# Ten up pairs ahead of the gate rows, three behind them, and two pairs gated out of their staging tiles

## The reference

```
sc = einsum("bshpc,hpnc->bshpn", q, sub_keys)        # scores of two key halves
v1, i1 = top_k(sc[..., 0, :], 16);  v2, i2 = top_k(sc[..., 1, :], 16)
top, ci = top_k(v1[..., :, None] + v2[..., None, :], 16)
idx = i1[ci // 16] * 128 + i2[ci % 16];  g = softmax(top)
a = einsum("td,ted->te", x, u[idx])
out = einsum("te,ted->td", g * gelu(a), v[idx])
```

## Time and profile before

| | |
|---|---|
| median of 3 runs | 4096.4 us (4095.26 to 4104.18) |
| the profiled execution | 4095.76 us, span 4093.7 us |
| PE busy | 3953.3 us, 97% of the span |
| DVE, ACT, POOL busy | 68%, 43%, 28% |
| mean granted TensorE clock | 0.985 of full |

### The profile page before, as it was taken

How to read it: one execution, slowest core, us unless ns; L and a number is a source line. 1 busy time by engine, 2 the same in 40 slices (tenths; PEclk the granted TensorE clock), 3 DMA queues, 4 the chain that set the end, 5 groups by cost and what they waited for, 6 DMA issues and landing times.

```text
span 4093.7 us, 59435 instructions
## 1 busy us (share of the span) xinstructions
PE 3953.3 (97%) x19746; PEld 3399.3 (83%) x19746; DVE 2796.2 (68%) x4541; ACT 1748.0 (43%) x3160; POOL 1153.4 (28%) x786
## 2 busy tenths in 40 slices
PE   7999999989999999999999999999899999999998
PEld 6677887789999988887866778877899999888886
DVE  2584351698887977777736843427988879677786
ACT  3533123225666654333346321322356666444343
POOL 1014563411211432222200155733011224222231
PEclk9999999999999999999999999999999999999999
DMA  3112332237877999999721122312478879999995
GB/s 125 48 64 81 104 104 70 95 106 249 297 283 280 392 375 345 347 347 343 275 77 48 62 92 103 119 57 89 152 245 291 289 281 405 371 345 349 347 357 183
DMA packets 360976, 879.48 MB, mean 215 GB/s; under 512 B 27856, under 2 KB 191952, under 8 KB 353872
## 3 DMA queue, kind: packets, MB, share of 16 engines
q1 hardware_dynamic: 153360, 508.21, 34.8%
q0 software_dynamic: 73728, 268.47, 17.2%
q10 hardware_dynamic: 133696, 100.67, 8.2%
HBM read 774.48 MB, written 102.76 MB: 214 GB/s over the span
## 4 chain that ended last, share of the span: by engine, by line
PE 77%; DVE 10%; DMA 3%; issue 3%; DVEq 2%; ACTq 2%; ACT 2%; POOL 0%; SPq 0%; POOLq 0%
PE ps L1223 44%; PE ps L1533 21%; PE ps L1510 3%; DMA raw<-in_experts 2%; PE ps L1236 1%; PE ps L1244 1%; ACTq L507 1%; PE ps L1285 1%; DVE wlo L807 1%; DVE acc L1092 1%; DVE ubuf L1085 1%; DMA act_e<-early_gelu 1%; PE ps L1303 1%; PE ps L1296 1%; PE ps L1295 1%
## 5 line engine op out<-in xcount | busy, mean ns | idle before, releaser
L1223 PE MATMUL ps<-xhi,whi 128*128 128x384 f32 (+1 forms) x3264 | 1189.7, 364 | 42.0 <-DVE inds L1070 14.0
L1223 PE MATMUL ps<-xlo,whi 128*128 128x384 f32 (+1 forms) x3264 | 1164.1, 357 | 0.0
L1223 PE MATMUL ps<-xhi,wlo 128*128 128x384 f32 (+1 forms) x3264 | 1164.1, 357 | 0.0
L476 ACT ACTIVATE whi<-raw 128x1024 fp32r<-128x1024 f32 x666 | 698.3, 1054 | 362.8 <-PE ps L1533 268.9
L807 DVE TENSOR_TENSOR wlo<-raw,whi 128x1024 fp32r<-128x1024 f32 x512 | 622.2, 1218 | 161.0 <-ACT whi L476 156.9
L1223 PEld LDWEIGHTS ps<-xhi,whi 128*128 128x128 f32 x3264 | 618.0, 189 | 100.2 <-issue 36.8
L1223 PEld LDWEIGHTS ps<-xlo,whi 128*128 128x128 f32 x3264 | 618.1, 189 | 51.0 <-issue 5.3
L1223 PEld LDWEIGHTS ps<-xhi,wlo 128*128 128x128 f32 x3264 | 616.9, 189 | 48.9
L1533 PE MATMUL ps<-whi,eh 128*128 128x512 f32 x1536 | 601.6, 392 | 26.3 <-DVE el L1184 26.1
L436 POOL DMA_INDIRECT ubuf<-in_up_rows,gidx x256 | 290.6, 1135 | 1100.6 <-DVE small L1085 913.2
L1533 PE MATMUL ps<-whi,el 128*128 128x512 f32 x1536 | 599.8, 391 | 0.0
(11 more groups left out here) (216 smaller groups left out, 4879.3 us busy)
## 6 DMA issues: line engine op xcount, KB each, us to landing
raw<-in_experts SPq DMA_DIRECT2D x512, 512.0 KB, 6.4
raw<-in_back SPq DMA_DIRECT2D x112, 512.0 KB, 3.2
gate_table<-gbuf SPq DMA_DIRECT2D x48, 1024.0 KB, 6.6
act_e<-early_gelu ACTq DMA_DIRECT2D x128, 384.0 KB, 7.2
gtile<-gate_table ACTq DMA_DIRECT2D x30, 1536.0 KB, 23.3
raw<-in_front SPq DMA_DIRECT2D x64, 512.0 KB, 3.2
raw<-in_gates SPq DMA_DIRECT2D x48, 512.0 KB, 3.2
early_gelu<-weighted SPq DMA_DIRECT2D x128, 192.0 KB, 5.2
```

What stands on the lines that cost most here:

```text
L476: A(whi[:, SLOT[s]:SLOT[s] + 1024], raw[:, SLOT[s]:SLOT[s] + 1024], ACT.Copy).then_inc(rounded[s], 1)
L1223: ins = MM(out, w[:, a:a + P], x[:, c, t0:], start=(i == 0 and n == 0), stop=(i == len(chunks) - 1 and n == 2))
```

## The change

`LEAD` goes from 12 to 10, and three pairs instead of one follow the last block (`EARLY - 3`, `EARLY - 2`, `EARLY - 1`), so the gate rows come two pairs sooner. The panels of up weights are rotated by two pairs on the host, so that the last two up pairs, 62 and 63, are down pairs 0 and 1. They are neither stored nor loaded: DVE multiplies them with the gates straight out of `weighted` and of `early0`/`early1`. ACT rounds the first product (`round_share`) between the Gelus of pairs 62 and 63, and PE computes pair 63 into banks 0 and 1. SP's gate store now comes ahead of the early stores of its iteration.

```diff
-LEAD = 12
+LEAD = 10
+HELD = 2
+STORED = EARLY - HELD
+assert LEAD % 2 == 0 and LEAD + DB * BLOCK + 3 == EARLY
...
+        def up_bank(i, m):
+            return {EARLY - 1: 0}.get(i, 4) + m
...
-                        eng.dma_start(early_d[2 * i + m], early(i, m)).then_inc(...)
+                        eng.dma_start(early_d[2 * (i + HELD) + m], early(i, m)).then_inc(...)
...
                 for i in range(EARLY):
                     for m in range(2):
                         stream(2 * i + 4 + m)
-                    if i:
-                        store_early(i - 1)
                     b, k = divmod(i - LEAD - 3, BLOCK)
                     if i >= LEAD + 3 and k < HALVES and k % 2 == 0:
                         store_gates(b * GROUPS + k // 2)
-                store_early(EARLY - 1)
+                    if 1 <= i <= STORED:
+                        store_early(i - 1)
                 for s in range(4):
-                    eng.wait_ge(early_stored[s], (L + 1) * (EARLY // 2 * 16))
+                    eng.wait_ge(early_stored[s], (L + 1) * (STORED // 2 * 16))
...
                 for i in range(LEAD):
                     early_pair(i)
-                    if i == 2 or i == LEAD - 3:
+                    if i == 2 or i == LEAD - 2:
                         pick_weights(int(i > 2))
-                    if i == LEAD - 2:
-                        pick_turn(1)
+                pick_turn(1)
...
                         load_gates(L * 0, 0, 22, 24)
-                        load_acts(L * 0, 0)
                         load_gates(L * 0, 1)
-                        load_acts(L * 0, 1)
-                        early_pair(i + HALVES + 1)
+                        load_acts(L * 0, HELD)
+                        load_acts(L * 0, HELD + 1)
+                early_pair(EARLY - 3)
+                early_pair(EARLY - 2)
+                round_share(L * 0, 0)
+                early_pair(EARLY - 1)
...
-                for m in range(2):
-                    hold(early_stored[m], (L + 1) * (EARLY // 2 * 16))
                 for r in range(PAIRS):
...
+                    if r == 0:
+                        for m in range(2):
+                            hold(early_ready[m], (L + 1) * EARLY - 1)
+                        TT(by_group(weighted[:, :, :]), by_group(weighted[:, :, :]), gates, ALU.mult).then_inc(w_ready, 1)
+                    elif r == 1:
+                        for m in range(2):
+                            dve.wait_ge(early_ready[m], (L + 1) * EARLY)
+                            ins = TT(by_group(weighted[:, m:m + 1, :]), by_group(early_odd[m][:, :].unsqueeze(1)), gates[:, m:m + 1], ALU.mult)
+                        ins.then_inc(w_ready, 1)
...
-                with pe.Fori(0, LEAD // 2 - 1) as i:
+                with pe.Fori(0, LEAD // 2) as i:
                     for k in range(2):
                         early_pair(i * 2 + k, k, i)
-                early_pair(LEAD - 2, 0, LEAD // 2 - 1)
                 turn(1)
-                early_pair(LEAD - 1, 1, LEAD // 2 - 1)
...
-                early_pair(EARLY - 1, 1, EARLY // 2 - 1)
+                early_pair(EARLY - 3, 1, EARLY // 2 - 2)
+                early_pair(EARLY - 2, 0, EARLY // 2 - 1)
                 pe.wait_ge(g_copied, (L + 1) * (DB * P // 4))
-                for m in range(2):
-                    pe.wait_ge(early_ready[m], (L + 1) * EARLY)
+                early_pair(EARLY - 1, 1, EARLY // 2 - 1, up_bank(EARLY - 1, 0))
```

More of the change, by code:

```diff
@@ L358, in store_early @@
                         eng.wait_ge(early_ready[m], L * EARLY + (i + 1))
-                        eng.dma_start(early_d[2 * i + m], early(i, m)).then_inc(early_stored[2 * (i % 2) + m], 16)
+                        eng.dma_start(early_d[2 * (i + HELD) + m], early(i, m)).then_inc(early_stored[2 * (i % 2) + m], 16)
                 def store_gates(y):
@@ L687, in early_pair @@
                         panel(n % 4, L, FIRST + n // 4)
-                        act.wait_ge(early_stored[n % 4], (L * (EARLY // 2) + i // 2) * 16)
-                        A(early(i, m), ps[:, 4 + m, 0:DT], ACT.Gelu).then_inc(early_ready[m], 1)
+                        act.wait_ge(early_stored[n % 4], (L * (STORED // 2) + i // 2) * 16)
+                        A(early(i, m), ps[:, up_bank(i, m), 0:DT], ACT.Gelu).then_inc(early_ready[m], 1)
                         round_panel(n % 4, L, FIRST + n // 4 + 1)
@@ L754, in _, with round_share @@
                         load_gates(L * 0, 0, 22, 24)
-                        load_acts(L * 0, 0)
                         load_gates(L * 0, 1)
-                        load_acts(L * 0, 1)
-                        early_pair(i + HALVES + 1)
+                        load_acts(L * 0, HELD)
+                        load_acts(L * 0, HELD + 1)
+                def round_share(j, r):
+                    act.wait_ge(w_ready, L * PAIRS + j * STEPS + (r + 1))
+                    A(eh[:, r % 2, :, :], weighted[:, :, :], ACT.Copy).then_inc(eh_ready, 1)
+                early_pair(EARLY - 3)
+                early_pair(EARLY - 2)
+                round_share(L * 0, 0)
+                early_pair(EARLY - 1)
                 def steps(j, first, last):
@@ L767, in steps @@
                                 round_panel(s, L, j * (STEPS // 2) + (FIRST + PAIRS // 2 + r // 2))
-                        act.wait_ge(w_ready, L * PAIRS + j * STEPS + (r + 1))
-                        A(eh[:, r % 2, :, :], weighted[:, :, :], ACT.Copy).then_inc(eh_ready, 1)
-                        if first and r == 2:
+                        if not (first and r == 0):
+                            round_share(j, r)
+                        if first and r == HELD:
                             for m in range(4):
-                                act.wait_ge(early_stored[m], (L + 1) * (EARLY // 2 * 16))
+                                act.wait_ge(early_stored[m], (L + 1) * (STORED // 2 * 16))
                             act.nop(nofuse=True)
-                        if not last or r + 2 < STEPS:
+                        if not (first and r < HELD or last and r + 2 >= STEPS):
                             load_acts(j, r + 2)
@@ L1163, in _ @@
                         pick_shares(b + 2, eidx[:, 2, :]).then_inc(pick_ready, 1)
-                for m in range(2):
-                    low(2 * (EARLY - 1) + m)
+                for n in range(2 * (LEAD + DB * BLOCK), 2 * EARLY):
+                    low(n)
                 def by_group(x):
                     return x.rearrange("p m (h t) -> p m h t", t=16)
-                for m in range(2):
-                    hold(early_stored[m], (L + 1) * (EARLY // 2 * 16))
                 for r in range(PAIRS):
                     k, q = r % 2, r // 4 % 2
+                    gates = gtile[q][:, :, 2 * (r % 4):2 * (r % 4) + 2, :].rearrange("p h m t -> p m h t")
                     drain()
-                    dve.wait_ge(act_loaded[k], (L * (PAIRS // 2) + r // 2 + 1) * 16)
                     dve.wait_ge(gt_loaded[q], (L * (PAIRS // 8 + 2 * (1 - q)) + (2 * (1 - q) + r // 8 + 1)) * 16)
-                    TT(by_group(weighted[:, :, :]), by_group(act_e[:, k, :, :]),
-                       gtile[q][:, :, 2 * (r % 4):2 * (r % 4) + 2, :].rearrange("p h m t -> p m h t"), ALU.mult).then_inc(w_ready, 1)
+                    if r == 0:
[7 more added lines that the diff above has]
+                        ins.then_inc(w_ready, 1)
+                    else:
+                        dve.wait_ge(act_loaded[k], (L * (STORED // 2) + r // 2) * 16)
+                        TT(by_group(weighted[:, :, :]), by_group(act_e[:, k, :, :]), gates, ALU.mult).then_inc(w_ready, 1)
                     new = range(e, SEL_EARLY + (SEL - SEL_EARLY) * (r + 1) // PAIRS)
@@ L1477, in _, with early_pair @@
                     ins.then_inc(xt_turned, 1)
-                def early_pair(i, parity, use):
+                def early_pair(i, parity, use, bank=4):
                     for m in range(2):
                         pe.wait_ge(early_ready[m], L * EARLY + i)
-                        linear(2 * parity + m, L, FIRST + use, ps[:, 4 + m, 0:DT], xhi, xlo, t0=GT)
+                        linear(2 * parity + m, L, FIRST + use, ps[:, bank + m, 0:DT], xhi, xlo, t0=GT)
                 def turn(t):
@@ L1596 @@
     L = LAYERS
-    u_v = rows(a["peer_u"].transpose(0, 2, 1)), a["peer_v"].reshape(L, NK, P, D)
+    u_v = np.roll(rows(a["peer_u"].transpose(0, 2, 1)), -2 * HELD, axis=1), a["peer_v"].reshape(L, NK, P, D)
     experts = np.concatenate(u_v, axis=1)
```

1 line of the change is left out of this document (removed).

## The result

The changed kernel takes 4107.2 us (median of 10 runs, 4102.7 to 4116.1) where the kernel before takes 4096.8 in the same comparison (10 runs, 4089.5 to 4106.0). The ratio is 1.0031, with a 95% interval of [1.0018, 1.0043], which is 7 to 18 us. The forecast was 4094.0, and the range ended at 4105.

What follows compares the result with a forecast made beforehand. TensorE, busy 97% of the span, was taken as the bound, so only its waits and lower clock counted. Terms -22.7 + 11.0 + 9.4 = -2.3 us from the 4096.4 median gave 4094, range 4079 to 4105.

Steps and rivals of the forecast that it cites:

- The switch: Up to down phase: TensorE's waits for `el`, 9.05 and 8.88 us, both go, gaining 17.9 us.
- The 4.8 us of clock: After the up-to-down turn: TensorE's half clock following the idle time disappears, gaining another 4.8 us over both layers.
- The second rival: Posed with the experiments: the down phase is worse off than before and sets the loss; no chance given.
- The lead: First up pairs: DVE's `low` of pair 9 now follows the last `pick`, so TensorE ends pair 9 later.
- the term of 11.0: Cost at the front: pair 9 ends 6.3 us late in layer 1 and 4.7 in layer 2, paid in full.
- the clock is absorbed: Before pair 9: clock lost through new short waits costs nothing, since DVE's list sets that pair's end.
- The pairs behind the loads: End of the up phase: ACT stands in front of loads, so TensorE waits 3.0 us for pair 61's Gelu.
- the term of 9.4: Cost at the back: 3.0 us of wait and 1.7 of clock, 4.7 per layer; ends 0 and 13.
- ACT then issues four transfers as before: Before pair 61's Gelu: ACT's four load issues take 5.6 us, as in the old kernel.
- ACT is stuck: Before pair 62: ACT's blocked issue takes 9.79 us, not 4.01, giving 4107 in all; chance 0.14.
- -22.7: Total gain at the up-to-down turn: 17.9 us of waits plus 4.8 us of clock.
- The scattered waits: Down phases: `el` waits of 8.2 us can fall away or double whatever else happens; not in the sum.

Runs made afterwards that it cites:

- e8: The changed kernel run once more, unaltered, for a second profile: 4103.2 us, one run.
- e1: Changed kernel with ACT's wait for the last gate store and its four loads moved behind pair 61's Gelus: 4099.0 us against 4099.5, ratio 0.9994.
- e5: Changed kernel with the edits of e1 and e2 together: 4085.8 us against 4095.9 for the kernel before, ratio 0.9971.
- e6: Changed kernel with SP's old store order, gate store behind the early stores of its iteration: 4106.4 us against 4095.9, ratio 1.0027.
- e10: e5 with the two `act_e` loads moved behind the first round of gating: 4076.9 us against 4099.4 for the kernel before, ratio 0.9950.
- e4: Changed kernel with 12 pairs leading and one following, `act_e` loads behind the first product's rounding: 4091.3 us against 4099.5, ratio 0.9977.
- e11: The kernel before run once more, unaltered, for a second profile: 4097.1 us, one run.
- e7: Kernel before with only SP's order changed, gate store ahead of the early stores of its iteration: 4090.6 us against 4095.9, ratio 0.9981.
- e3: Kernel before with 10 pairs leading and three following, still gating from HBM with old store order: 4115.2 us against 4099.5, ratio 1.0046.
- e2: Changed kernel with each lead `low` behind the same `pick` call as in the kernel before: 4094.1 us against 4099.5, ratio 0.9984.

## Why the prediction was wrong

**The switch: right.** TensorE's first down product follows pair 63 with no wait and a clock of 1.00. The waits are gone as predicted (9.05 and 8.88 us). The 4.8 us of clock are real, too: take from each "down" its waits for `el` and what it lost at half clock (4.8 us behind the switches before, 1.7 elsewhere), and the kernel before has 1062.0 - 8.2 - 4.8 - 1.7 = 1047.3 left, the changed one, which lost 3.4 at half clock elsewhere, 1068.5 - 16.3 - 3.4 = 1048.8, its second profile 1057.4 - 9.5 = 1047.9. The same work costs the same within 1.5 us (within 3.5 us over all thirteen profiles, 1046.7 to 1050.2), and before the change 4.8 us of half clock came on top. The second rival falls with this, but for the waits for `el`.

**The lead: the mechanism right, the term of 11.0 too small.** The `low` of pair 9 was predicted for 957.2 and came at 957.04, and the Gelu behind pair 9 at 967.03 where I had 966.7 for TensorE's end. Counted from the first lead product, whose start differs between the profiles by 0.5 us in layer 1 and 6.9 in layer 2, the end of pair 9 is 7.2 us later (predicted 6.3) in layer 1 and 5.7 (4.7) in layer 2: 12.9 against 11.0. Two things make up the difference. From the start of the `low` to the end of pair 9 it took 10.0 us (957.04 to 967.0) and not 1.2 + 8.3 = 9.5, in both layers. And against the first lead product the `low` came 0.4 and 0.5 us later than DVE's list less the `low`s of two pairs. That the clock is absorbed there held: before pair 4 the wait was 4.85 us in the first profile of the changed kernel and 3.27 in its second (e8), and pair 9 started 92.1 and 92.0 us behind the first lead product.

**The pairs behind the loads: the mechanism right, the term of 9.4 too small.** The gate store took 9.7 us from issue to ACT's first load; the prediction's own numbers, from 1487.5 to 1497.0, make 9.5. The step that failed is "ACT then issues four transfers as before, which took 5.6 us". It took 7.1 us in layer 1 (1486.59 to 1493.69) and 7.3 in layer 2. They were not issued quite as before, either: both `act_e` loads now stand behind the 1,536 KB gate load, and before only one did. The wait before pair 62 was 3.77 and 5.14 us, where I had 3.0 twice (in layer 1 the gate store went out 13.7 us ahead of TensorE's end of pair 61, where I had 12.6, which took 1.1 us off again; in layer 2 it was 12.4). The clock took 1.7 and 2.3 and not 1.7 twice: 12.9 us. The rival "ACT is stuck" had the direction with a blocked issue of 9.79 us; the truth lay between it and the forecast. The prediction weighed a rule of the Trainium skill against the 4.01 us (DMA: Bandwidth & Descriptors, Queues, rings and completion order: each DMA engine goes round robin between the queues with work). By that rule, and by an even split, the issue would take about 8 us. The rows show 6.08 and 6.31 here, 7.0 to 7.7 in e1 and e5, 4.70 in e6 and 1.04 in e10. The trace agrees with the rule in its direction: the issue took longer than 4 us. That sharing with SP's queue is what lengthened it is not shown. The runs differ in what is under way beside the loads and in how far they stand behind the 1,536 KB gate load of their own queue (0.5 us, some 3 in e4 with an issue of 1.82 us, and 9.4 in e10), and none changes one of the two alone. Whatever the cause, this case belonged in the forecast and not beside it.

**The sum.** With the measured terms, -22.7 + 12.9 + 12.9 = +3.1 us, against -2.3 predicted and 7 to 18 measured. "Up" alone accounts for it without the switch's clock: -17.9 + 12.9 + 12.9 = +7.9, and the table shows +8.0. What the clock gave in "down", 4.8 us, does not show in the total. The waits for `el` inside "down" are the likeliest place. In the two second profiles (e8 and e11) "down" takes the same, 1057.4 and 1057.6: the kernel before has 4.7 us of half clock behind its switches, and the changed one 4.6 us more of these waits. They average 10.4 us in the eight profiles with the tiles and without a hold, and 7.3 in the five that wait at the switch. That is some 3 us more, but where two profiles of one kernel differ by 7 us it is not shown that the change brings them; nor is the rest of the difference, which the spread of "rest" (1719.0 to 1729.5 for the same code) is large enough to hide. So some 4 us between the terms' sum and the near end of the measured interval, and 7 us to its middle, stay open.

**The scattered waits: underrated.** I wrote that they "can fall away or double", put nothing for them in the sum, and put the range's upper end at 4105 all the same. With the two terms in their measured sizes the forecast would have been 4099.5 and its range would have had to reach past 4107, since one kernel's waits for `el` alone moved by 7 us between two profiles.

**Missed altogether:** that both costs sat in choices beside the change's idea. Gating the last two pairs from their tiles, with SP's new store order, is worth 0.23% without any pair moved (e4); the store order alone is worth 0.19% (e7), so what the tiles add can't be told from the times, though "up" is 7.2 us shorter with them (1273.1 against 1280.3). Moving two pairs from the lead to the end costs 0.46% (e3) as written; with the `low`s kept early and the loads behind the Gelus it neither costs nor gains anything that shows (e5's "up" is 1273.5, e4's 1273.1), and with the loads in two pieces the whole gains 0.50%.

## What to carry to other kernels

Moving work past an in-order queue is priced by where the other entries of that queue end up: here four loads in front of three pairs' Gelus instead of one, and the `low`s tied to the last call instead of to the pair that needs them. Before a wait is removed by a shorter lead or a longer tail, list for each engine what now stands between the late thing and its next consumer, and move that too; e1, e2 and e10 each move a few lines and together turn +0.31% into -0.50%. And do not carry a blocked issue's duration from one place to another: give it the range of all its rows, and put the middle into the sum.
